# Three groups of small products in each attention head, moved beside other small groups

## The reference

```python
def diff_attn_core(q, k, v, q_pos, k_pos, lam):
    s = jnp.einsum('bqhmd,bkhmd->bhmqk', q, k).astype(jnp.float32) * (DIFF_HEAD_DIM ** -0.5)
    visible = (k_pos[None, :] // CHUNK) <= (q_pos[:, None] // CHUNK)
    p = jax.nn.softmax(jnp.where(visible, s, NEG), axis=-1)
    a = p[:, :, 0] - lam * p[:, :, 1]
    return jnp.einsum('bhqk,bkhe->bqhe', a.astype(v.dtype), v)

def diff_post(o, g, lam_init):
    of = o.astype(jnp.float32)
    of = of * lax.rsqrt(jnp.mean(jnp.square(of), axis=-1, keepdims=True) + LN_EPS) * g * (1.0 - lam_init)
    ...
```

## Time and profile before

| | |
|---|---|
| median of 3 runs | 2132.62 us |
| the profiled execution | 2132.67 us, of which the span of its instructions is 2130.9 us |
| PE matmuls busy | 2116.2 us, 99% of the span |
| PE weight loads busy | 1935.2 us, 91% |
| DVE, ACT, POOL busy | 69%, 58%, 3% |
| one head in the trace | 27.5 us (from 178.4 to 205.9 us, the third head of layer 0) |

### The profile page before, as it was taken

The page is one execution under the profiler, slowest core; times in us unless marked ns, Lnnn a source line. Parts: engine busy times, 40 slices in busy tenths (PEclk is TensorE's granted clock), DMA queues, the critical chain, the costliest instruction groups (busy, mean ns, idle before and its releaser), DMA issues.

```text
span 2130.9 us, 38215 instructions
## 1 busy us (share of the span) xinstructions
PE 2116.2 (99%) x15004; PEld 1935.2 (91%) x15004; DVE 1472.1 (69%) x2336; ACT 1230.6 (58%) x2493; POOL 64.6 (3%) x100
## 2 busy tenths in 40 slices
PE   9999999999999999999999999999999999999998
PEld 8998889999989898989889888899999898989897
DVE  6857777766879356665667577786778793566656
ACT  4457776696535356656234577766965353556561
POOL 1000000001000000000001000000110001000000
PEclk9999999999999999999999999999999999999999
DMA  7887562487861855454368765524778527544541
GB/s 251 237 291 257 204 219 107 146 250 218 222 228 50 237 158 171 146 168 139 109 188 240 279 251 211 211 79 156 244 206 246 204 73 224 166 165 154 168 149 70
DMA packets 100867, 399.27 MB, mean 187 GB/s; under 512 B 15273, under 2 KB 16937, under 8 KB 87601
## 3 DMA queue, kind: packets, MB, share of 16 engines
q1 hardware_dynamic: 67904, 191.55, 26.4%
q0 software_dynamic: 7936, 92.28, 17.1%
q10 hardware_dynamic: 24848, 112.99, 14.8%
HBM read 367.42 MB, written 118.23 MB: 228 GB/s over the span
## 4 chain that ended last, share of the span: by engine, by line
PE 96%; DMA 2%; ACT 1%; DVE 1%; issue 0%; ACTq 0%; DVEq 0%
PE PS L828 9%; PE PS L830 9%; PE PS L829 9%; PE PS L1049 6%; PE PS L1051 6%; PE PS L1050 6%; PE PS L917 5%; PE PS L919 5%; PE PS L918 5%; PE PS L863 4%; PE PS L862 4%; PE PS L861 4%; PE PS L987 3%; PE PS L988 3%; PE PS L989 3%; PE PS L1177 2%
## 5 line engine op out<-in xcount | busy, mean ns | idle before, releaser
L828 PE MATMUL PS<-xt_hi,w_hi 128*128 128x320 f32 x1184 | 382.3, 323 | 0.2
L830 PE MATMUL PS<-xt_hi,w_lo 128*128 128x320 f32 x1184 | 365.9, 309 | 0.0
L829 PE MATMUL PS<-xt_lo,w_hi 128*128 128x320 f32 x1184 | 365.7, 309 | 0.0
L2541 DVE TENSOR_TENSOR w_lo<-w_raw,w_hi 128x1024 fp32r<-128x1024 f32 x146 | 177.5, 1222 | 151.0 <-ACT w_hi L1579 149.4
L2548 DVE TENSOR_TENSOR w_lo<-w_raw,w_hi 128x1024 fp32r<-128x1024 f32 (+1 forms) x176 | 199.3, 1138 | 114.8 <-ACT w_hi L1595 114.5
L1579 ACT ACTIVATE w_hi<-w_raw 128x1024 fp32r<-128x1024 f32 x146 | 153.6, 1059 | 178.5 <-PE PS L1051 152.6
L828 PEld LDWEIGHTS PS<-xt_hi,w_hi 128*128 128x128 f32 x1184 | 222.8, 188 | 5.4 <-issue 4.3
L829 PEld LDWEIGHTS PS<-xt_lo,w_hi 128*128 128x128 f32 x1184 | 223.0, 188 | 0.1
L830 PEld LDWEIGHTS PS<-xt_hi,w_lo 128*128 128x128 f32 x1184 | 222.3, 188 | 0.0
L1595 ACT ACTIVATE w_hi<-w_raw 128x1024 fp32r<-128x1024 f32 (+1 forms) x176 | 172.2, 984 | 86.1 <-PE PS L989 66.3
L1049 PE MATMUL PS<-w_hi,act_a_hi 128*128 128x512 f32 x480 | 187.9, 391 | 2.3 <-DVE rows L3007 2.3
(11 more groups left out here) (391 smaller groups left out, 5095.0 us busy)
## 6 DMA issues: line engine op xcount, KB each, us to landing
w_raw<-in_weights SPq DMA_DIRECT2D x186, 512.0 KB, 4.8
kc<-in_k_cache ACTq DMA_DIRECT2D x32, 1024.0 KB, 7.7
vc<-in_v_cache ACTq DMA_DIRECT2D x16, 2048.0 KB, 8.7
w_raw<-up_sums SPq DMA_DIRECT2D x112, 256.0 KB, 2.9
up_sums<-in_up_blocks POOLq DMA_DIRECT2D x24, 1024.0 KB, 9.0
w_raw<-in_up_blocks SPq DMA_DIRECT2D x84, 256.0 KB, 2.8
down_sums<-in_down_blocks POOLq DMA_DIRECT2D x16, 1024.0 KB, 11.3
w_raw<-in_down_blocks SPq DMA_DIRECT2D x32, 512.0 KB, 3.4
```

Of the source, the lines that this page charges most:

```text
L828: mm(out, wh, hi[:, k, c], start=(k == 0), stop=False)
L829: mm(out, wh, lo[:, k, c], start=False, stop=False)
L830: last = mm(out, wl, hi[:, k, c], start=False, stop=(k == KT - 1))
L2541: v.tensor_tensor(w_lo[slot][:], raw[:, raw_of(s, n)[0], :], w_hi[slot][:].bitcast(F32), ALU.subtract)\
```

## The change

Three groups of each head are moved in PE's program; the programs of the other engines are the same, and so is every product.
1. `unit_product` of unit 2 goes from the end of the head, after the last tile, to step 1 of the next head's first tile (or of the gate tile in `last_head_end`), just ahead of `unit_transpose` of unit 3, which stood there already.
2. `dec_transposes` of group 0 goes from step 2 of the third tile to the place ahead of that tile, right behind `output_transposes`. Group 1 goes from step 5 to step 4.
3. `dec_map_sum` goes from step 4 of the last tile to step 5, between `unit_product` of units 0 and 1 and `unit_transpose` of unit 2.

```diff
-                tile(0, 0, None if first else {(0, 1): lambda: unit_transpose(l, h - 1, (3,)),
+                tile(0, 0, None if first else {(0, 1): lambda: (unit_product(l, h - 1, (2,)),
+                                                                unit_transpose(l, h - 1, (3,))),
                                                (0, 6): lambda: mean_squares(n - 1)})
...
                 if not first:
                     output_transposes(l, h - 1, 7)
-                tile(1, 0, {(0, 2): lambda: dec_transposes(l, h, 0), (0, 5): lambda: dec_transposes(l, h, 1)})
+                dec_transposes(l, h, 0)
+                tile(1, 0, {(0, 4): lambda: dec_transposes(l, h, 1)})
                 dec_products(l, h)
                 unit_score(l, h, p, (3,))
                 unit_transpose(l, h, (0, 1))
-                tile(1, 1, {(1, 4): lambda: dec_map_sum(l, h),
-                            (1, 5): lambda: (unit_product(l, h, (0, 1)), unit_transpose(l, h, (2,)))})
-                unit_product(l, h, (2,))
+                tile(1, 1, {(1, 5): lambda: (unit_product(l, h, (0, 1)), dec_map_sum(l, h),
+                                             unit_transpose(l, h, (2,)))})
 
             def last_head_end(l):
-                early_gate(l, 2, 0, {(0, 1): lambda: unit_transpose(l, HEADS - 1, (3,)),
+                early_gate(l, 2, 0, {(0, 1): lambda: (unit_product(l, HEADS - 1, (2,)),
+                                                      unit_transpose(l, HEADS - 1, (3,))),
                                      (0, 6): lambda: mean_squares(l * HEADS + HEADS - 1)})
```

## The result

The changed kernel takes 2141.18 us (median of 6 runs, 2139.41 to 2143.3), beside 2132.41 us for the kernel before on the same chip: a ratio of 1.0037, with a 95% interval of 1.0022 to 1.0052, so 4.7 to 11.1 us slower. 10.2 us were forecast (2142.9). Both programs timed once more, in another set, gave 2138.54 beside 2130.46 us, 1.0042 (1.0028 to 1.0057). In that set a further timing of the kernel before has one run of 11995 us, which its ratio leaves out.

The account below looks back on a forecast made before the run. PE was taken as the bound, its matmuls filling 2116.2 of 2130.9 us. Terms 9.0 + 1.3 - 0.1 = 10.2 us on 2132.67 gave 2142.9 us; own range 2141.6 to 2143.9, stated range 2138.7 to 2145.0 (0.86).

Parts of the forecast that it names:

- What a group alone costs: Small groups on PE, 48 in all: joining gives about nothing, at most 0.2 us, taken as 0.1 us.
- The early transposes: Group 0's fifth transpose waits for ScalarE's output copy: 0.64 us in each of 14 heads, 9.0 us (8.1 to 9.6).
- The weight load: The fifth transpose's weight load waits too, adding 0.06 us (0 to 0.104); done during the wait, 8.1 instead of 9.0.
- What unit 2's product covered: At each layer's end, PE's wait for the gate's copy loses unit 2's product as cover: 0.66 us twice, 1.3 us.
- The other moved waits: The other moved groups on PE still come behind what they need; no new wait, group 1 at 195.5 against 194.84.
- The sum: All terms together: 9.0 + 1.3 - 0.1 = 10.2 us slower, 2142.9 us.
- The rival that was faster: Joining pays 0.085 us for each of 48 groups and ScalarE's copy is in time: 2128.6 us; chance 0.04.
- joining that pays beside the wait: Joining pays 4.1 us while the wait at the early transposes stands: 2138.8 us; chance 0.08.
- the delay is given back later: PE's waits outside the heads, 2.3 and 1.8 us, shrink by up to 4.1 us: 2138.8; chance 0.05.
- What would show it: Profile signs: 14 waits at L1122 of about 0.6 us, gate wait 0.66 us longer twice, joined starts 0.11 us apart.

Follow-up runs that it names:

- e2: The kernel before with only the second part of the change (samples' transposes moved early): 2139.13 us beside 2130.93, ratio 1.0036.
- e5: The change, but group 0 of the samples' transposes at step 1 of the third tile, behind three large products: 2134.03 us beside 2131.51, ratio 1.0010.
- e6: The change, with unit 0's exponentials ahead of the output copy on ScalarE: 2148.41 us in one run.
- e4: The change, but in each layer's last head unit 2's product is back ahead of the product waiting for the gate's copy: 2139.99 us, ratio 1.0039.
- e3: The change, but group 0's fifth transpose alone stands at step 2 of the third tile: 2133.06 us beside 2130.93, ratio 1.0009.
- e1: The change with its second part undone, samples' transposes inside the third tile again (steps 2 and 5): 2130.28 us beside 2130.93, ratio 1.0000.
- e8_best: e3's change with group 1 at step 5, and unit 2's product and unit 3's transposes ahead of the gate at layer end: 2130.03 us beside 2131.51, 0.9991.
- e7: The change with its second part undone and the map sum ahead of the products of units 0 and 1: 2131.78 us in one run.

## Why the prediction was right, point by point

- **What a group alone costs:** right for the full-width groups. Unit 2's product and unit 3's transposes, which stood apart, take 0.67 us and 0.44 us joined as well. Wrong in size for the map sum: 0.05 us is saved in each head, 0.04 in the head's length, 0.6 to 0.7 us in all, where the forecast took 0.1 for all joining. The term rested on four records that take as long as records twice as wide; it was not seen that what follows the last of them counts.
- **The early transposes:** 0.64 us forecast, 0.65 by the starts in one place, 0.66 in the head of e2; 14 of them are 9.2 us (9.0 forecast). The pieces came out singly: the fifth transpose comes 0.58 us late (0.58 forecast), which includes the 0.05 us from the copy's end to its start (0.06 forecast), and from it to the next product but one it takes 0.07 us more than without a wait (0.06 forecast, as its weight load). e5 and e6 moved the cover and the copy, and the wait followed by the same amount.
- **The weight load:** the load of the fifth transpose starts with it, at 192.36 after 0.66 us of idleness, in all 14 heads, as the prediction has it. But where the prediction says that the trace doesn't agree with the Trainium skill, it read too much into such a row. The Trainium skill (TensorE: Matmul & The Clock Gate, "Part 2: What happens when you issue a matmul") says that weight loads are pulled ahead of products in flight when their row groups don't conflict or the load goes to a background buffer. In the records of the trace the wait for `a_done` stands on the load itself, and so does the gate's; none of the 160 transposes at L1122 carries a wait. So the load is held together with its transpose, and the row says nothing against the rule. A load that isn't held goes ahead, as the rule has it: in a layer's first head, where `a_done` is long raised, the load of the fifth transpose starts 0.11 us ahead of it, while the record of the fourth (0.27 us) still runs.
- **What unit 2's product covered:** 1.3 us forecast, 1.3 by e4 against the change. From the last large product to the released one it takes 1.10 us with unit 2's product between (e4) and without it (the change).
- **The other moved waits:** none appeared in the change, as forecast: in the heads with a predecessor group 1 starts about 0.7 us behind the end of group 0's copy. In e3, where group 0 is complete only two steps ahead, it waited.
- **The sum:** 9.2 + 1.3 - 0.7 = 9.8 us by the pieces, 10.0 by the heads of the trace, 10.2 forecast, 8.8 by the medians. The rival that was faster fell at `a_done`, as it was stated; joining that pays beside the wait fell with e1 (a head of 27.44 us, not 27.3). That the delay is given back later was not seen, but not ruled out for a microsecond or two.
- **What would show it:** "about 0.6 us each" in the list of waits was the wrong reading: it shows 0.43, for 0.65 us lost. The records of the joined groups start 0.11 us apart, as said, but for the step from the map sum's first record to its second (0.06 us, in the kernel before as well).

## What to carry to other kernels

On an engine that is full, small work between large work need not cost anything by itself: count a group together with what it does to its neighbours before joining it to another. Before a group is moved, list for each of its instructions what it waits for and how much work stands between the wait's cause and it; the work that stood in the gaps here covered two copies on another engine. If only the last instruction of a group waits, it can stay behind alone (e8_best), provided that what follows keeps its own distance.

## What the runs showed of the hardware that was not expected

- Two float32 products of 64 columns (four records) cost 0.05 us less with transposes behind them than with products or large products behind them (e7 against the change).
- The same program's waits outside the heads, for VectorE's rows and a transfer of cached keys, were 4.1 us in one profiled execution and absent in another, with the same mean granted clock (0.999).
- At the start of an execution a large product took 0.27 us from start to start up to 10.6 us (before) or 0.15 us from 5.9 us on (the change); the record of the full granted clock begins at 10.6 and at 5.8 us.
- A wait is written ahead of a transpose, but the trace has it on the weight load: in the change 48 of the 160 loads at L1122 carry a wait and none of the 160 transposes does, and the loads held by `a_done` start 0.66 us after the load before them has ended, with their transposes.
